# Later modulation weights through two ring slots, and TensorE multiplying constants while it waits before the expert loop

## What is computed

```python
mod = silu([c_ctx, c]) @ w_mod + b_mod          # (2, 6144): shift1, scale1, gate1, shift2, scale2, gate2
h = rms_norm(x, g1) * (1 + scale1) + shift1
proj = h @ w_in                                  # 3200 columns
mix = concat(attention(proj), rwkv7(proj), hgrn2(proj))
x = x + gate1 * (mix @ w_out)
h = rms_norm(x, g2) * (1 + scale2) + shift2
logits = h @ router_w + router_b                 # 32 experts, top 4, softmax gates
x = x + gate2 * moe(h)                           # w_gu (32, 1024, 2048), w_down (32, 1024, 1024)
y = rms_norm(x, g)
```

## Time and profile before

| | before |
|---|---|
| median of 3 runs | 1332.73 us (1329.97 to 1333.65) |
| profiled execution | 1328.41 us |
| its span | 1326.3 us |
| TensorE matmul busy | 1188.8 us (90%) |
| weight loads, TensorE | 482.8 us (36%) |
| VectorE / ScalarE / GpSimd busy | 314.2 / 228.8 / 37.9 us |
| mean TensorE clock | 0.964 |
| HBM read | 457.96 MB, 346 GB/s over the span |
| chain that ended last | DMA 52%, PE 41%, DVE 3%, ACT 3% |

### The profile page before, as it was taken

How to read it: one execution, slowest core, us unless ns; L and a number is a source line. 1 busy time by engine, 2 the same in 40 slices (tenths; PEclk the granted TensorE clock), 3 DMA queues, 4 the chain that set the end, 5 groups by cost and what they waited for, 6 DMA issues and landing times.

```text
span 1326.3 us, 17258 instructions
## 1 busy us (share of the span) xinstructions
PE 1188.8 (90%) x7106; PEld 482.8 (36%) x7106; DVE 314.2 (24%) x633; ACT 228.8 (17%) x381; POOL 37.9 (3%) x69
## 2 busy tenths in 40 slices
PE   3987998888599999999999999999999999999994
PEld 1333576774433333333332333333323333333331
DVE  1202657453411111211111121111111211111113
ACT  2111253532211111111111111111111111111112
POOL 0400000000000000000000000000000000000000
PEclk9998999699689999999999999999999999999998
DMA  9977200228549999999999999999999999999991
GB/s 372 322 283 273 98 1 3 73 97 346 197 190 427 427 428 429 428 429 429 425 430 427 428 427 428 427 427 427 426 428 427 427 427 428 428 429 426 429 428 71
DMA packets 44240, 459.93 MB, mean 347 GB/s; under 512 B 5112, under 2 KB 7328, under 8 KB 16432
## 3 DMA queue, kind: packets, MB, share of 16 engines
q1 hardware_dynamic: 41152, 451.98, 81.4%
q0 software_dynamic: 2576, 6.35, 1.7%
q10 hardware_dynamic: 480, 1.13, 0.2%
HBM read 457.96 MB, written 1.47 MB: 346 GB/s over the span
## 4 chain that ended last, share of the span: by engine, by line
DMA 52%; PE 41%; DVE 3%; ACT 3%; issue 1%; SPq 0%; DVEq 0%; ACTq 0%
DMA ring<-in_moe_w_gu_dram 46%; PE bank L1158 15%; DMA ring<-in_w_mod_dram 5%; PE bank L1178 4%; PE bank L568 4%; PE bank L961 2%; PE bank L682 2%; PE bank L545 1%; PE bank L1121 1%; PE bank L1136 1%; PE bank L558 1%; PE bank L667 1%; PE bank L1148 1%; PE bank L928 1%; ACT L1228 1%
## 5 line engine op out<-in xcount | busy, mean ns | idle before, releaser
L1158 PE MATMUL bank<-ring,proj 128*64 128x512 f32 x2048 | 458.6, 598 | 33.2 <-DMA ring<-in_moe_w_gu_dram 33.2
L1158 PEld LDWEIGHTS bank<-ring,proj 128*64 128x64 f32 x2048 | 140.3, 137 | 350.1 <-issue 275.0
L1178 PE MATMUL bank<-ring,proj 128*64 128x512 f32 x1024 | 233.9, 598 | 11.9 <-DVE proj L2048 11.9
L2039 DVE TENSOR_SCALAR proj<-bank 128x512 f32<-128x512 f32 x32 | 22.1, 692 | 480.6 <-PE bank L1158 480.6
L1515 ACT ACTIVATE proj<-proj 128x512 f32<-128x512 f32 x32 | 20.2, 630 | 604.4 <-DVE proj L2039 604.4
L1178 PEld LDWEIGHTS bank<-ring,proj 128*64 128x64 f32 x1024 | 69.1, 136 | 131.8 <-issue 131.8
L568 PE MATMUL bank<-ring,hT 128*128 128x512 f32 (+2 forms) x224 | 92.0, 567 | 4.5 <-DVE hT L1848 2.7
L2051 DVE COPY proj<-bank 128x512 f32<-128x512 f32 x32 | 22.1, 691 | 249.1 <-PE bank L1178 249.1
L1121 PE MATMUL bank<-h_nat,proj 128*64 128x512 f32 x264 | 64.0, 607 | 0.0
L1136 PE MATMUL bank<-proj 64*128 64x512 f32 x256 | 63.6, 615 | 0.0
L568 PEld LDWEIGHTS bank<-ring,hT 128*128 128x128 f32 x224 | 42.9, 195 | 50.9 <-issue 40.7
(11 more groups left out here) (330 smaller groups left out, 791.6 us busy)
## 6 DMA issues: line engine op xcount, KB each, us to landing
ring<-in_moe_w_gu_dram SPq DMA_DIRECT2D x128, 2048.0 KB, 24.4
ring<-in_moe_w_down_dram SPq DMA_DIRECT2D x64, 2048.0 KB, 21.7
ring<-in_w_mod_dram SPq DMA_DIRECT2D x12, 2048.0 KB, 8.9
ring<-in_w_in_dram SPq DMA_DIRECT2D x5, 2048.0 KB, 17.3
ring<-in_w_out_dram SPq DMA_DIRECT2D x2, 2048.0 KB, 8.4
const_sb<-in_constants_dram POOLq DMA_DIRECT2D x1, 2450.0 KB, 14.7
ring<-in_w_in_dram SPq DMA_DIRECT2D x1, 1536.0 KB, 7.3
ring<-in_w_in_dram SPq DMA_DIRECT2D x1, 1024.0 KB, 5.6
```

The lines of the kernel that those rows point to most:

```text
L1158: mm = pe.matmul(b[CAP * half:CAP * half + CAP, :], xT[:, k % 4, k // 4, :], ring[:, j, 2048 * kc + o + 512 * half:2048 * kc + o + 512 * h ...
L1178: mm = pe.matmul(b_down[CAP * half:CAP * half + CAP, :], aT[:, k % 4, k // 4, :], ring[:, 4 + j, D * kc + 512 * half:D * kc + 512 * half + ...
L2039: ts(moe["glu"], bank[4][:, :], LIMIT, None, ALU.min).then_inc(sem("glu_sb"), 1)
```

## The change

The eight later modulation pieces go alternately through slots 4 and 5, each loaded when the piece two before it has been used. What lives in slot 5 moves out of the way: `t1` becomes a part of `sg_sample`, and GpSimd fills `X` and `Y` only after the last modulation (`mod_used` 12) and then clears `AKd` in VectorE's place; VectorE waits for that before it writes `AKd`. A new function `keep_busy(n)` issues n matmuls of 128x128 by 128x512 on constants into bank 7, which nobody reads: nine before TensorE waits for the second stream's `h2`, two before it waits for `chosen`, two before `end_phase`.

```diff
@@ -44,8 +44,8 @@
 ROT = 6
 
 FRONT = [("mod0", 0, 0), ("mod0", 1, 1), ("mod0", 2, 4), ("mod0", 3, 5), ("in", 0, 0), ("in", 1, 1), ("mod", 0, 4),
-         ("in", 2, 0), ("in", 3, 1), ("mod", 1, 4), ("mod", 2, 4), ("in", 4, 0), ("mod", 3, 4), ("mod", 4, 4),
-         ("in", 5, 1), ("mod", 5, 4), ("mod", 6, 4), ("in", 6, 0), ("mod", 7, 4), ("out", 0, 4), ("out", 1, 3)]
+         ("mod", 1, 5), ("in", 2, 0), ("in", 3, 1), ("mod", 2, 4), ("mod", 3, 5), ("in", 4, 0), ("mod", 4, 4), ("mod", 5, 5),
+         ("in", 5, 1), ("mod", 6, 4), ("mod", 7, 5), ("in", 6, 0), ("out", 0, 4), ("out", 1, 3)]
 FRONT_ROUNDS = [sum(slot == j for _, _, slot in FRONT) for j in range(NSLOT)]
 FRONT_AT = {}
 for kind, k, slot in FRONT:
@@ -394,7 +394,7 @@
                     lo, w = PIECES[k]
                     ring_load(slot, w_in[:, :, lo:lo + w])
                 if kind == "mod":
-                    sp.wait_ge(sem("mod_used"), 3 if k == 0 else 4 + k)
+                    sp.wait_ge(sem("mod_used"), 3 + k)
                     g, j = 1 + k // 4, k % 4
                     ring_load(slot, w_mod[:, 2 * j:2 * j + 2, 2048 * g:2048 * (g + 1)])
 
@@ -489,8 +489,9 @@
                     pool.tensor_copy(at[name].rearrange("p (a t) -> p a t", a=8), bc(eye, [P, 8, DH], 1)).then_inc(sem("rw_eye"), 1)
 
             pool.wait_ge(sem("const_in"), 16)
-            pool.wait_ge(sem("mod_used"), 4)
+            pool.wait_ge(sem("mod_used"), 12)
             unit_start(0)
+            pool.memset(at["AKd"], 0.0).then_inc(sem("ak_zero"), 1)
             pool.wait_ge(sem("at_keys"), 1)
             pool.dma_start(a["new_att_k"][0, 0].rearrange("g t d -> t g d"),
                            at["qn"][:, 512:640].rearrange("t (g d) -> t g d", g=2)).then_inc(sem("cache_out"), 16)
@@ -1083,7 +1084,14 @@
                 pe.wait_ge(sem("mixed"), s + 1)
                 turn_mix(s)
                 project_out(s)
-            for s in range(2):
+            def keep_busy(n):
+
+                for _ in range(n):
+                    pe.matmul(bank[7][:, :], ident, C("hg0")[:, 0:512], start=True, stop=True)
+
+            for s in range(2):
+                if s:
+                    keep_busy(9)
                 pe.wait_ge(sem("h2"), s + 1)
                 for part in range(2):
                     transposes(("h2T", s, part), [h[:, s, P * c:P * c + P] for c in range(4 * part, 4 * part + 4)])
@@ -1096,6 +1104,7 @@
                                    start=(c == 0), stop=(c == KC - 1))
             filled(mm, "router")
 
+            keep_busy(2)
             pe.wait_ge(sem("chosen"), 1)
             b = open_bank(pe, "pos")
             before = C("earlier")
@@ -1544,7 +1554,7 @@
             step = Steps(dve, "dve_step")
             powers = [0]
             kb, kd, t0 = (ap.rearrange("p (d n) -> p d n", d=2) for ap in (mix[:, 1, 0:512], mix[:, 1, 512:1024], mix[:, 0, 512:1024]))
-            t1 = at["t1"]
+            t1 = sg_sample[:, 0:256]
             two = [P, 2, 256]
             lbt = Pm("lb")
 
@@ -1661,6 +1671,7 @@
                 for q in range(2):
                     after(dve, "rw_b", s, q)
                 dve.copy_predicated(Y, bc(merge(0, False).bitcast(I32), [P, 2, 4, DH], 2), LRd[:, :, :, 0, :]).then_inc(sem("rw_Y0"), 1)
+                dve.wait_ge(sem("ak_zero"), 1)
                 keep_lower("rw_k", AKd)
 
             def rw_level_w(s, k):
@@ -1849,8 +1860,7 @@
                        mT[:, part, c, 1:2], ALU.mult, ALU.add).then_inc(sem("hT_sample"), 1)
                 dve.wait_ge(sem("hT_sample"), 4 * part + 4)
                 done(dve.nop(), "xT", 1, part)
-            dve.memset(h_t[:, 0:1024], 0.0)
-            step(dve.memset(at["AKd"], 0.0))
+            step(dve.memset(h_t[:, 0:1024], 0.0))
 
             project(0)
             keys = rw_keys()
```

## The result

| | before | after |
|---|---|---|
| median | 1331.4 us (1329.97 to 1333.65, 4 runs) | 1310.82 us (1307.18 to 1312.27, 4 runs) |
| ratio | | 0.9837, 95% interval 0.9816 to 0.9858 |
| profiled execution, span | 1328.41, 1326.3 us | 1311.34, 1309.6 us |
| mean TensorE clock | 0.964 | 0.975 |

The change saves 20.6 us where 13.6 were forecast: 1310.82 us lies just under the range (1311 to 1326). The first thing to see is that the two profiled executions differ by less, 17.1 us, than the two medians. The execution of before that was profiled was the shortest shown, the one of after was the second slowest of its four.

A forecast was written before the change was run, and what follows sets the result against it. The DMA paces the expert loop, which starts when TensorE has used expert 0's first slot, so its chain up to there counts. Front 7.1 plus pre-loop 6.5 us: 1331.4 - 13.6 = 1317.8 us, range 1311 to 1326.

The forecast's parts named there:

- Rival 5: Expert loop: the DMA-bound loop absorbs the change, which does nothing on time; chance 0.02.
- The waits for modulation weights: Front: all five TensorE waits go, 11.2 us, plus 1.7 us of slow clock, together 12.9 us saved.
- The load moved ahead: Front: the earlier modulation load delays the third `w_in` piece by 5.0 us, plus 0.8 us of slow clock.
- The cover: Front: VectorE's slack before the last modulation falls from 3.58 to 1.0 us, so it is not late.
- GpSimd: After the last modulation: its moved copies and clearing of `AKd` have 11.7 us before VectorE needs them; cost nothing.
- the nine: Wait for the second `h2`: constant matmuls take 8.02 of 8.07 us; full clock saves 3.9 us in transposes and router.
- The pairs and the gather: Before the expert loop: pairs of 1.8 us fit their waits; `pos` gives 0.3, gate transposes 0.3, gather 1.8 us.
- Rival 3: Before the loop: the clock falls under the router's matmuls, some 2 of 6.5 us are left, 1323 us; chance 0.10.
- Line 1196: Down biases ahead of the loop: 4.17 us, mostly at full clock already, give 0.5 us, between 0 and 0.7.
- The first slot: Expert 0: the clock falls again under the down biases, so its first slot stays at 5.5 us; no saving counted.
- Rival 1: First expert: the clock stays up, first slot 3.5 instead of 5.5 us, 2.9 us more saved, 1315 us; chance 0.15.
- Rivals 2 and 4: Front gives only 2.5 to 3 us, 1322 us, chance 0.12; constant matmuls run at 1.2 GHz, slower, chance 0.04.

The follow-up runs named there:

- e6: The changed kernel with five more constant matmuls ahead of the third `w_in` piece; 1309.42 us, ratio to before 0.9812.
- e5: The changed kernel with the second later modulation piece loaded behind the third `w_in` piece instead of ahead of it; 1306.31 us, ratio to before 0.9798.
- e9: The changed kernel with the edits of e5 and e8, and down-bias matmuls of 128 rows, 96 of them cleared; 1301.63 us, ratio to before 0.9767.
- e1: The changed kernel without its constant matmuls, so with the two ring slots alone; 1320.55 us, ratio to before 0.9915.
- e4: The changed kernel's own code once more, on the same chip as its parts; 1310.09 us, ratio to before 0.9834.
- e7: The changed kernel with the four down-bias matmuls replaced by constant ones of 128 rows, down biases missing from the result; 1308.42 us, ratio to before 0.9811.
- e8: The changed kernel with four constant matmuls ahead of TensorE's wait for `kh` in the mixers; 1306.63 us, ratio to before 0.9801.
- e3: The kernel before with only the nine constant matmuls ahead of the second `h2`; 1327.60 us, ratio to before 0.9968.
- e2: The kernel before with all the constant matmuls (9, 2, 2) but without the ring slots; 1322.05 us, ratio to before 0.9924.

## Why the prediction was wrong

**The bound held.** The prediction said: "Every microsecond by which TensorE finishes expert 0's first slot sooner comes off the end in full": 16.7 us there, 17.1 us in the profiled executions, and 907.8 against 908.2 us from there on. Rival 5 is out. The 7.0 us between 13.6 and 20.6 split in two halves. 3.5 us lie between the forecast and the two profiled executions: 2.2 in the front, 0.8 in the mixers, 0.1 in the last stage and 0.4 behind it. The other 3.5 us lie between these executions and the medians.

**The waits for modulation weights: right.** 11.2 us of waits are gone, with the 1.7 us of slow clock; no other wait came up.

**The load moved ahead: the step that was mis-sized in the front.** I said "So the DMA is full there, and 2048 KB more at 418 GB/s are 5.0 us". The piece came 3.2 us later, not 5.0, within the bounds but below the value taken. In all six traces with the change's order (with e6) TensorE's wait for it ends between 70.9 and 71.4 us; with the load behind it (e5, e9) at 67.85 and 66.93. The DMA share on which I leaned counts an engine as busy while it moves little. Windows of before, then of after:

```profile
44.00:46.00 2.00, 2.00 (x6) 0.89 (x5) 0.00 (x0) 0.30 (x1) 2.00 (x4) 1.00 0.84 188
46.00:48.00 2.00, 2.00 (x6) 0.95 (x5) 0.00 (x0) 0.00 (x0) 2.00 (x4) 1.00 0.89 116
48.00:50.00 2.00, 2.00 (x6) 0.82 (x5) 0.00 (x0) 0.00 (x0) 2.00 (x4) 1.00 1.09 120
```

```profile
44.00:46.00 2.00, 2.00 (x6) 0.95 (x5) 0.00 (x0) 0.38 (x1) 2.00 (x5) 1.00 1.04 420
46.00:48.00 2.00, 2.00 (x6) 0.88 (x5) 0.00 (x0) 0.00 (x0) 2.00 (x4) 1.00 1.04 410
48.00:50.00 2.00, 2.00 (x6) 0.83 (x5) 0.00 (x0) 0.00 (x0) 2.00 (x4) 1.00 1.03 363
50.00:52.00 2.00, 2.00 (x6) 0.95 (x5) 1.24 (x3) 0.00 (x0) 0.48 (x1) 1.00 1.22 147
52.00:54.00 2.00, 2.00 (x6) 0.87 (x5) 1.86 (x5) 0.00 (x0) 0.00 (x0) 1.00 0.91 210
```

Before, shares of 0.84 to 1.09 carry 188, 116 and 120 GB/s, at a time when GpSimd's queue issues its small loads. After, the same windows carry 420, 410 and 363 GB/s, 1.5 MB more in 6 us. Part of this only changes places: a slow stretch follows from 50 to 54 us, with 147 and 210 GB/s where before had 372 and 423. By 68 us after has moved 1.0 MB more than before; the rest of the load's 2.1 MB is what the piece waits for, some 3 us at the 355 to 390 GB/s there. The clock's extra cost was right, 9.58 - 8.83 = 0.75 us against 0.8. With 3.2 in place of 5.0 the front's sum is 12.9 - 3.2 - 0.75 = 9.0 us, and the traces have 9.3. Over all traces the last modulation starts at 144.1 us with one slot (five traces) and at 133.3 us with two (after, e1, e4, e7, e8): 10.8 us, of which 1 us is again the first trace's luck. The mixers let this gain through: they take 162.1 to 165.3 us in the five traces, and 161.5 to 164.1 us in after, e1, e4 and e7.

**The cover, GpSimd, the nine: right.** Slack 0.92 us for 1.0; the three GpSimd instructions hidden; 7.89 us for 8.02.

**The pairs and the gather: right as read.** Between the two traces, transposes and router gave 4.0 us (3.9 in the sum), `pos` up to the gate transposes 0.5 (0.3), the gate transposes 0.1 (0.3), the gather 1.8 (1.8) and line 1196 0.5 (0.5); the last stage fell by 6.6 us against 6.5 forecast. Rival 3 happened in part: the clock fell under the router's matmuls, but it was back behind the pair. `pos` begins 6.98 us behind the start of the router's group, against 6.63 in e3, so this cost 0.35 us and not 4.

**Line 1196: the term of the sum that failed.** "Line 1196 (4.17 us) ran mostly at full clock already (0.79 in 370 to 375); I take 0.5 us, between 0 and 0.7." In three of four traces without fillers it takes 7.19 us, and with them 3.7, so the term is 3.5 us in these three and 0.5 only in the first. The mistake is in what was read, not in the mechanism: a stage whose clock changes from execution to execution was priced from one execution, and that one was the shortest shown by 1.6 us. I noted that and corrected the sum's base to 1331.4, but not the terms, so that the base was a typical execution and the savings were those of a lucky one. 10.8 in the front and 9.6 in the last stage make 20.4 us, or 19.1 with the mean of all six traces; measured are 20.6 and 21.1. How often an execution pays the 7.19 us rests on four traces; why the clock rises early in some and late in others stays open.

**The first slot: right, and now shown.** The clock falls at the down biases with 32 rows, in spite of a TensorE busy without a gap, and e7 takes the fall away with matmuls of the same size and 128 rows of other operands; e9, with the real operands and 96 cleared rows beside them, has the same gain (64.67 us). Rival 1 did not happen in the change (1.98 us bias, 15.45 us first expert). The Trainium skill says in "TensorE: Matmul & The Clock Gate", section "What's actually happening", that the clock follows how busy the PE has been recently. e7 shows the limit of this: two kernels, equally busy in 352 to 356 us, 3.69 and 3.70 us, differ in the clock behind it.

**Rivals 2 and 4.** The front gave more, not less. The slower case, fillers at 1.2 GHz, did not come in the median, but e8's profiled execution has a mild form of it: the second pair took 3.76 us, and 4.6 us were lost from the first pair to the down biases.

## What to carry to other kernels

Where TensorE waits for another engine in a stage on the critical path, constant matmuls that fit the wait cost nothing here and gave full clock to what followed in most traces. They should bridge every wait of the stage: e3, with the two later waits left open, kept 3.6 of e2's 9.2 us. Take such a stage's price from several executions, or bound it by its rows at 1.2 and at 2.4 GHz, since one trace may show a lucky one. And look at bytes per second beside the busy share before calling the DMA full; in e5 the load did better behind the piece that is needed next.

## What the runs showed that I had not expected

- Equal time, unequal rows: behind four matmuls of 32 rows (3.69 us) the clock falls, behind four of 128 rows, with 96 rows of weights zero in e9, it stays (e7 and e9: 64.4 and 64.7 us against 67.4). And in the mixers of after, TensorE is busy for all 12 us from 236 to 248 us, mostly with matmuls of 64 rows, at a clock of 0.50 throughout.
- Fillers shorten the stage in most executions but don't make it safe: 67.37 to 67.43 us in four traces, 68.55 and 74.39 us in two more, against 73.99 to 78.76 us without them.
- A DMA share of 1.09 at 120 GB/s in the one kernel, and of 1.03 at 363 GB/s in the other, in the same 2 us.
